# A two-block transformer in one kernel: two-pass gated P times V, gate/up's start and end reordered, context spread, own first buffers for down

## The reference

```
x = x + concat(pool_mixer(u), gla_mixer(q, k, v, g, a), fox_mixer(q, k, v, f)) @ w_o
# fox_mixer: p = softmax(q k^T / 8 + F_t - F_s, causal); o = p @ v   (8 heads of 64)
h = rmsnorm(x, ln2)
gate, up = split(h @ w_gu)              # 1024 -> 2 x 2816
x = x + (silu(gate) * up) @ w_down
x = rmsnorm(x, ln_f)
# second block: adaptive modulation from c, and differential attention over
# 256 context rows (their own modulation) and the 1024 rows of x; final rms norm
```

## Time and profile before

| what | us |
|---|---|
| median of 3 runs | 2244.05 (2243.75 to 2244.96) |
| the profiled execution's own time | 2245.73 |
| its span, first to last instruction | 2243.9 |
| PE busy | 2113.5 (94% of the span) |
| DVE busy | 1384.7 (62%) |
| ACT busy | 1046.0 (47%) |
| POOL busy | 768.8 (34%) |
| mean granted PE clock | 0.977 of full speed |

### The profile page before, as it was taken

The page is one execution under the profiler, slowest core; times in us unless marked ns, Lnnn a source line. Parts: engine busy times, 40 slices in busy tenths (PEclk is TensorE's granted clock), DMA queues, the critical chain, the costliest instruction groups (busy, mean ns, idle before and its releaser), DMA issues. The chain is left out here.

```text
span 2243.9 us, 29580 instructions
## 1 busy us (share of the span) xinstructions
PE 2113.5 (94%) x10092; PEld 1726.2 (77%) x10092; DVE 1384.7 (62%) x1856; ACT 1046.0 (47%) x1677; POOL 768.8 (34%) x503
## 2 busy tenths in 40 slices
PE   6999999988989999989999989999999999999798
PEld 5887777767767888878787868878778787877687
DVE  5545545435577665565445467777867687786864
ACT  4434545445233322322234345566666666665651
POOL 2211222256265554444344533222223122222420
PEclk9999999999999999999999999999999999999899
DMA  3110000004223333243444541111010111102312
GB/s 117 43 38 29 10 28 28 19 19 169 85 85 130 113 122 107 85 144 129 153 148 144 180 174 66 38 38 38 28 51 23 42 42 37 37 28 72 125 66 94
DMA packets 59366, 175.53 MB, mean 78 GB/s; under 512 B 7568, under 2 KB 7984, under 8 KB 59168
## 3 DMA queue, kind: packets, MB, share of 16 engines
q1 hardware_dynamic: 55728, 161.81, 20.7%
q0 software_dynamic: 3568, 12.81, 1.7%
HBM read 144.44 MB, written 29.89 MB: 78 GB/s over the span
## 5 line engine op out<-in xcount | busy, mean ns | idle before, releaser
L2929 ACT ACTIVATE diff_probs<-psum,diff_neg_max 128x1280 f32<-128x1280 f32 x128 | 170.3, 1330 | 121.9 <-DVE diff_neg_max L3159 120.8
L3159 DVE TENSOR_REDUCE diff_neg_max<-psum 128x1 f32<-128x1280 f32 x128 | 189.5, 1486 | 48.7 <-PE psum L2479 48.6
L2538 PE MATMUL psum<-h_hi,w_hi 128*128 128x512 f32 x480 | 193.4, 403 | 7.8 <-DVE h_lo L1523 4.7
L2539 PE MATMUL psum<-h_lo,w_hi 128*128 128x512 f32 x480 | 190.3, 396 | 0.0
L2540 PE MATMUL psum<-h_hi,w_lo 128*128 128x512 f32 x480 | 189.6, 395 | 0.0
L2799 POOL TENSOR_SCALAR diff_probs<-diff_probs,diff_recip 128x1280 f32<-128x1280 f32 x64 | 86.0, 1344 | 268.5 <-DVE diff_probs L3176 268.5
L2210 DVE TENSOR_TENSOR down_a_lo<-down_feat,down_a_hi 128x512 fp32r<-128x512 f32 x42 | 100.1, 2383 | 115.3 <-ACT down_a_hi L2111 114.6
L395 PE MATMUL psum<-h_hi,w_hi 128*128 128x512 f32 x368 | 153.7, 418 | 4.7 <-POOL w_lo L384 2.7
L1651 POOL TENSOR_TENSOR gu_p_lo<-gu_p_whole,gu_p_hi 128x512 fp32r<-128x512 f32 x84 | 125.2, 1513 | 86.3 <-ACT gu_p_hi L1643 86.3
L2478 PE MATMUL psum<-diff_k_hi_lo,diff_q_hi_twice 128*128 128x512 f32 (+1 forms) x384 | 142.8, 372 | 11.6 <-ACT diff_probs L2929 11.5
L1976 POOL TENSOR_TENSOR w_lo<-down_w_raw,w_hi 128x1024 fp32r<-128x1024 f32 x42 | 101.0, 2407 | 140.3 <-ACT w_hi L2109 140.3
(11 more groups left out here) (448 smaller groups left out, 5708.5 us busy)
## 6 DMA issues: line engine op xcount, KB each, us to landing
down_w_raw<-in_w_down SPq DMA_DIRECT2D x44, 512.0 KB, 3.6
gu_w_next<-in_w_gu SPq DMA_DIRECT2D x42, 512.0 KB, 4.2
w_whole<-in_da_w_in SPq DMA_DIRECT2D x30, 512.0 KB, 3.5
gu_ada_w<-in_ada_w SPq DMA_DIRECT2D x24, 512.0 KB, 3.6
w_whole<-in_w_in SPq DMA_DIRECT2D x23, 512.0 KB, 3.4
kept_hid<-gu_hid SPq DMA_DIRECT2D x44, 256.0 KB, 2.1
down_feat<-kept_hid SPq DMA_DIRECT2D x44, 256.0 KB, 4.0
diff_rope_half<-in_rope SPq DMA_DIRECT2D x17, 512.0 KB, 4.1
```

Of the source, the lines that this page charges most:

```text
L2538: pe.matmul(out, wh, rh, start=(k == 0), stop=False)
L2539: pe.matmul(out, wh, rl, start=False, stop=False)
L2929: act.activation(dst, core.psum[:, 1536 * z:1536 * z + NKEY], ACT.Exp, bias=nm[:, qb % 2, z:z + 1], accum_out=rs[:, qb % 2, z:z + 1]).then ...
L3159: dve.tensor_reduce(nm[:, qb % 2, z:z + 1], core.psum[:, 1536 * z:1536 * z + NKEY], AX.X, ALU.max, negate=True).then_inc(s[f"max{z}"], 1)
```

## The change

It has five parts.

1. `times_v` has two matmuls in place of three. v is laid out so that the 128 columns of a head are its 64 hi and 64 lo columns (`v_of`). Both are multiplied with P_hi and with P_lo, so that the product v_lo x P_lo is added. The sum stands in two sets of 64 rows, and `output` copies one and adds the other: a second DVE instruction, with a wait between.
2. Start of gate/up. DVE makes tile 1's weight sums after the rests of the last turn. POOL's order becomes p1, p6, p5, s1, p7, p2, p3, s4, p4. SP stores tile 0 first, then loads tile 2's weights, then the condition rows and the first modulation weights. `cond_silu` moves behind `silu_of_first`; DVE's wait for it moves to tile 2.
3. The context: ACT's eight roundings go to tiles 15, 16 and 17 (3, 3, 2), DVE's to tiles 16, 17 and 18 (2, 3, 3), SP's four stores stand after tile 19.
4. Down's first two weight tiles get buffers of their own, over those of s1 (used by p5), so that ACT rounds them, and DVE takes their features' rests, inside the last tile of gate/up.
5. `add` of token tiles 0 to 2 waits for that token tile's own last matmul (`s_sum`), and no longer for the whole half.

The diff, with most unchanged lines left out:

```diff
@@ -423,7 +423,11 @@
         v_at = next_place(nc)
-        v = [ph.sb(n, [P, NT, P], F32R) for n in ("v_hi", "v_lo")]
+        v = ph.sb("v_hi_lo", [P, 2 * SEQ], F32R)
+        v_parts = v[:, :].rearrange("p (t q m) -> p t q m", t=NT, q=4)
+        v_hi_part = lambda j: v_parts[:, 4 * j:4 * j + 4, 0:4:3, :]
+        v_lo_part = lambda j: v_parts[:, 4 * j:4 * j + 4, 1:3, :]
+        v_of = lambda h, kt: v[:, (2 * kt + h) * P:(2 * kt + h + 1) * P]
...
@@ -481,7 +485,7 @@
-        gates_hi = v[1][:, :, :].rearrange("p t m -> p (t m)")
+        gates_hi = v[:, SEQ:2 * SEQ]
...
@@ -503,7 +507,7 @@
         names = ("parts gates_hi gate_rows k_copied consts_r staged q_hi k_hi q_done k_done v_turned v_hi v_done f_rows "
-                 "scored maxed probs recips scaled pt_turned pt_hi pt_lo pv_done o_read feat_hi")
+                 "scored maxed probs recips scaled pt_turned pt_hi pt_lo pv_done o_rest o_read feat_hi")
...
@@ -735,7 +739,7 @@
                     act.wait_ge(s["v_turned"], 2 * n + j + 1)
-                    act.activation(v[0][:, 4 * j:4 * j + 4, :], ps[PIECE_BANK][:, :].rearrange("p (t m) -> p t m", t=4),
+                    act.activation(v_hi_part(j), ps[PIECE_BANK][:, :].rearrange("p (t h m) -> p t h m", t=4, h=2),
...
@@ -1001,8 +1005,8 @@
                     dve.wait_ge(s["v_hi"], 2 * n + j + 1)
-                    dve.tensor_tensor(v[1][:, 4 * j:4 * j + 4, :], ps[PIECE_BANK][:, :].rearrange("p (t m) -> p t m", t=4),
-                                      v[0][:, 4 * j:4 * j + 4, :].bitcast(F32), ALU.subtract).then_inc(s["v_done"], 1)
+                    dve.tensor_tensor(v_lo_part(j), ps[PIECE_BANK][:, :].rearrange("p (t h m) -> p t h m", t=4, h=2),
+                                      v_hi_part(j).bitcast(F32), ALU.subtract).then_inc(s["v_done"], 1)
...
@@ -1023,8 +1027,11 @@
                     dve.wait_ge(s["pv_done"], nth_pt(i, h, g, nkt[g] - 1) + 3)
-                    r = slice(h * DH, (h + 1) * DH)
-                    dve.tensor_copy(mix[r, 4 + i, g * HALF:(g + 1) * HALF], ps[O_BANK][r, :]).then_inc(s["o_read"], 1)
+                    r, rest = slice(h * DH, (h + 1) * DH), slice((1 - h) * DH, (2 - h) * DH)
+                    out = mix[r, 4 + i, g * HALF:(g + 1) * HALF]
+                    dve.tensor_copy(out, ps[O_BANK][rest, :]).then_inc(s["o_rest"], 1)
+                    dve.wait_ge(s["o_rest"], i * 4 + h * 2 + g + 1)
+                    dve.tensor_tensor(out, ps[O_BANK][r, :], out, ALU.add).then_inc(s["o_read"], 1)
...
@@ -1291,10 +1298,8 @@
                     hi, lo = turned_hi(g, kt)[:, c0:HALF], turned_lo(g, kt)[:, c0:HALF]
-                    pe.matmul(out, v[0][:, kt, :], hi, start=(kt == 0), stop=False)
-                    pe.matmul(out, v[0][:, kt, :], lo, start=False, stop=False)
-                    pe.matmul(out, v[1][:, kt, :], hi, start=False, stop=(kt == nkt[g] - 1))\
-                      .then_inc(s["pv_done"], 1)
+                    pe.matmul(out, v_of(h, kt), hi, start=(kt == 0), stop=False)
+                    pe.matmul(out, v_of(h, kt), lo, start=False, stop=(kt == nkt[g] - 1)).then_inc(s["pv_done"], 1)
...
@@ -1776,6 +1781,8 @@
                         for j, n in enumerate(("hi", "lo")))
+    first_wh, first_wl = (over(f"down_first_w_{n}", [P, 2, D], mix_at + (32 + 8 * j) * 1024, F32R)
+                          for j, n in enumerate(("hi", "lo")))
...
@@ -1851,15 +1858,18 @@
         sync.dma_start(ctx[:, :, :], d["ctx"].rearrange("t p n -> p t n")).then_inc(s_cx, 16)
-        sync.wait_ge(qp.s["prepared"], qp.prepared("s3_lo"))
-        sync.dma_start(cond[:, :, :], d["cond"].partition_broadcast(P)).then_inc(s_cond, 16)
-        load_ada(0)
         qp.store_first(sync, 0)
+        qp.store_second(sync, 0)
...
         def tile(i, last=False):
-            qp.store_second(sync, i - 1)
+            if not (isinstance(i, int) and i == 1):
+                qp.store_second(sync, i - 1)
...
                 qp.load(sync, i + 1)
+            if isinstance(i, int) and i == 1:
+                sync.wait_ge(qp.s["prepared"], qp.prepared("s3_lo"))
+                sync.dma_start(cond[:, :, :], d["cond"].partition_broadcast(P)).then_inc(s_cond, 16)
+                load_ada(0)
...
@@ -1867,15 +1877,14 @@
             tile(i)
-        with sync.Fori(TWICE.stop, CTX_AT + 2) as i:
+        with sync.Fori(TWICE.stop, CTX_AT + 5) as i:
...
             sync.dma_start(d["o_feat"][4 + j, :, :], part.rearrange("p k n -> p (k n)")).then_inc(s_hc_st, 16)
-        with sync.Fori(CTX_AT + 2, LAST_TILE) as i:
-            tile(i)
+        tile(CTX_AT + 5)
...
@@ -1948,7 +1957,7 @@
         whole_rows(6)
-        for q in qp.ORDER[:4]:
+        for q in qp.ORDER[:3]:
...
@@ -1958,9 +1967,13 @@
         rest_s("p5", 2)
+        for q in ("p7", "p2", "p3"):
+            qp.rest_w(pool, 1, q)
         rest_s("p3", 3)
-        qp.rest_w(pool, 1, "p2")
-        with pool.Fori(1, LAST_TILE) as i:
+        qp.rest_w(pool, 1, "p4")
+        for q in qp.ORDER[:5]:
+            qp.rest_w(pool, 2, q)
+        with pool.Fori(2, LAST_TILE) as i:
...
@@ -1971,7 +1984,7 @@
                 for b in range(2):
-                    hi, lo = weights(g, last, b)
+                    hi, lo = weights(g, first, last, b)
...
@@ -1983,9 +1996,10 @@
-    def weights(g, last, b):
-
-        return (last_wh[:, b, :], last_wl[:, b, :]) if g and last else (core.wh[:, b, :], core.wl[:, b, :])
+    def weights(g, first, last, b):
+
+        wh, wl = (last_wh, last_wl) if g and last else (first_wh, first_wl) if first and not g else (core.wh, core.wl)
+        return wh[:, b, :], wl[:, b, :]
...
@@ -2058,6 +2072,8 @@
                 qp.round_w(act, i + 1, "p2")
+            if isinstance(i, int) and i == 1:
+                cond_silu(act)
...
@@ -2073,42 +2089,47 @@
-        def ctx_hi(act):
+        def ctx_hi(act, part):
             act.wait_ge(s_mods, MODS_DONE)
-            for k in range(KT):
+            for k in part:
...
-        tile(1, cond_silu)
+        tile(1)
...
             tile(i)
-        tile(CTX_AT, ctx_hi)
-        with act.Fori(CTX_AT + 1, LAST_TILE) as i:
+        tile(CTX_AT, lambda act: ctx_hi(act, range(0, 3)))
+        tile(CTX_AT + 1, lambda act: ctx_hi(act, range(3, 6)))
+        tile(CTX_AT + 2, lambda act: ctx_hi(act, range(6, KT)))
+        with act.Fori(CTX_AT + 3, LAST_TILE) as i:
             tile(i)
-        tile(LAST_TILE)
+        def first_hi(act):
+            act.wait_ge(s_hc_st, 64)
+            act.wait_ge(qp.s["done"], qp.nth(LAST_TILE, "p5"))
+            for b in range(2):
+                act.wait_ge(loaded[b], 32)
+                act.activation(weights(0, True, False, b)[0], raw[:, b, :], ACT.Copy).then_inc(whi, 1)
+                act.activation(features(0, False, b)[0], feat[:, b, :], ACT.Copy).then_inc(ahi, 1)
+
+        tile(LAST_TILE, first_hi)
...
-        act.wait_ge(s_hc_st, 64)
...
                     n = g * FT + 2 * i + b
-                    hi = features(g, last, b)[0]
                     if g == 0 and first:
-                        act.wait_ge(loaded[b], 32)
-                        act.activation(hi, feat[:, b, :], ACT.Copy).then_inc(ahi, 1)
-                        act.wait_ge(qp.s["done"], qp.nth(LAST_TILE, "p4"))
+                        continue
...
                         act.wait_ge(mm, n + 1)
-                    act.activation(weights(g, last, b)[0], raw[:, b, :], ACT.Copy).then_inc(whi, 1)
-                    if not (g == 0 and first):
-                        act.activation(hi, feat[:, b, :], ACT.Copy).then_inc(ahi, 1)
+                    act.activation(weights(g, first, last, b)[0], raw[:, b, :], ACT.Copy).then_inc(whi, 1)
+                    act.activation(features(g, last, b)[0], feat[:, b, :], ACT.Copy).then_inc(ahi, 1)
...
@@ -2120,8 +2141,10 @@
-        if t >= 4:
-            dve.wait_ge(s_sum, t - 3)
+        if t == 3:
+            dve.wait_ge(mm, FT + 2)
+        else:
+            dve.wait_ge(s_sum, t + 1 if t < 3 else t)
...
@@ -2183,12 +2206,11 @@
             dve.tensor_scalar(yn[:, t % 2, :], y[:, t, :], ss[:, c], None, ALU.mult).then_inc(tr.ready, 1)
-            if t == NT - 1:
-                qp.sums_of_weights(dve, 1)
...
                 tr.dve(dve, t)
+        qp.sums_of_weights(dve, 1)
...
@@ -2241,6 +2263,8 @@
                 qp.second_half(dve, i - 1)
+                if isinstance(i, int) and i == 2:
+                    dve.wait_ge(qp.s["s_hi"], S_HI_COND)
...
@@ -2249,8 +2273,6 @@
                 modulate(first_ada(i) + 1)
-            if first:
-                dve.wait_ge(qp.s["s_hi"], S_HI_COND)
...
@@ -2277,10 +2299,10 @@
-        def ctx_lo(dve):
+        def ctx_lo(dve, part):
...
             dve.wait_ge(s_mods, MODS_DONE)
-            for k in range(KT):
+            for k in part:
...
@@ -2303,13 +2325,14 @@
         tile(CTX_AT)
-        tile(CTX_AT + 1, ctx_lo)
-        with dve.Fori(CTX_AT + 2, LAST_TILE) as i:
+        tile(CTX_AT + 1, lambda dve: ctx_lo(dve, range(0, 2)))
```

(16 more changed lines are left out.)

## The result

The changed kernel took 2217.12 us in the median of 4 executions (2213.17 to 2226.13), the kernel before 2244.51 beside it (2243.75 to 2246.56): ratio 0.9882, 95% interval 0.9848 to 0.9917, 27 us faster. The forecast was 2207 with a range of 2197 to 2220. The profiled execution took 2213.54, its span 2211.6 at a mean clock of 0.983; against the profile before that is 32.3 us less span.

A forecast was written before the change was run, and what follows sets the result against it. TensorE was taken as busy nearly always, leaving fewer matmuls or its waits and the half clock behind them to win. 8.3 + 11.0 + 10.8 + 5.3 + 1.4 = 36.8 off 2244.05 gave 2207 us, range 2197 to 2220.

The forecast's parts named there:

- the 2200 to 2214: Whole kernel: the time range in us given to the forecast itself, chance 0.60.
- two rivals at 2215: Either fox gives nothing (chance 0.15), or gate/up's start keeps its waits and gives 3 us, not 11 (chance 0.10).
- Fox, 8.3: Attention heads: 96 matmuls removed, worth 17.3 us, of which 8.3 reach the end (2 to 14).
- The extra instruction: Fox: the added DVE add takes 0.7 us, mostly hidden, paid once in full before the barrier ending the stage.
- w_o, forecast at nothing: The w_o products after fox: the prediction had no term for them, 0 us.
- The start, 11.0: Start of gate/up: waits for last turn, s3's rest and tile 2's weights go or move, 11.0 us (8 to 14).
- The wait moved to p6: Start of gate/up: a wait of 4 to 5 us before p6, eleven half-clock matmuls costing 2.2, p6 starting 2.8 earlier.
- The context, 10.8: Gate/up's four context tiles: 11.1 us of excess goes except 0.3, giving 10.8 (7 to 11.1).
- Down's start, 5.3: Down's first step loses 8.5 us of excess; 2.7 wait at the third tile and 0.5 clock remain: 5.3 (3 to 6.5).
- The adds, 1.4: End of down's first half: three of four adds go ahead of the last matmul, 1.4 us (0 to 1.5).
- the rivals: Fox nothing 0.15; start keeps waits 0.10; all fox kept, no clock fall, 2196 us, 0.09; slower clock 0.04; within 0.2% 0.02.
- The clock did not fall for whole heads: Fox: rival that half clock stays for whole heads, a pair costing up to 69 us, two giving 2345; chance 0.04.

The follow-up runs named there:

- e6: The changed kernel without VectorE's second instruction for the output of P times V, only the half with v's high part copied: 2217.77 us in one execution.
- e5: The changed kernel with the second matmul of each key tile in P times V issued twice, so three matmuls again: 2225.47 us in one execution.
- e1: The kernel before with only the two-matmul P times V, its layout of v and second output instruction: 2239.0 us, ratio 0.9969.
- e4: The changed kernel with loads for down's third and fourth weight tiles ahead of gate/up's last stores, ln_f and x1 loads behind: 2209.99 us, ratio 0.9838.

## Why the prediction was right, and where it was not

The sign, and the range of 2197 to 2220, held. The forecast of 36.8 us stands against 32.3 in the profiles and 27 in the medians. The median of 2217 lies outside the 2200 to 2214 that I gave 0.60, and inside the range because this was drawn out for two rivals at 2215 that did not come. The total was also helped by misses that offset one another: fox and the start gave more than forecast, w_o and down's start less. In order of the parts:

**Fox, 8.3.** Right in size. The mean of the stage is 305.9 in four traces with three products and 295.15 in nine with two (e6 left aside); less the 1.0 of the gap, 9.8 are won. Kept in the first heads was 1.74 of 2.16, where I had 1.94. In the second heads 1.0 of 2.16 was kept where no half clock disturbs the comparison (38.94 to 37.96), and I had 0.4: part of it is lost there, as said, but less. That it is DVE that takes it was not tested. The profile before also stood on the long side of a scatter of 1.5 us for each change of pair, which I had not reckoned with. The extra instruction cost its 0.7 once, as forecast; the gap grew by 1.0 in all. The page "TensorE: Matmul & The Clock Gate" of the Trainium skill, section Back-to-back issue gap, would have made this term about 5; putting the matmuls back cost 9.8 (e5), so the trace's price stands.

**w_o, forecast at nothing.** The first step that failed. I costed the stage as untouched, but 96 matmuls and their weight loads less are a shorter program for TensorE, and one of its packets of instructions now falls among w_o's first weights. The loss came with the fewer matmuls (e1 has it) and went when they were put back (e5); it was 3.2 in the profile after, and 0 to 3 in others.

**The start, 11.0.** Measured 12.6 (11.3 alone). The wait moved to p6, as said: 4.3 where 4 to 5 was forecast. Counted from the last product of w_o, p6 began 2.65 earlier for my 2.8, with some nine matmuls about 0.42 apart behind it, which cost 1.7 for my 2.2, and tile 2 right behind tile 1. Each of the steps held.

**The context, 10.8.** 11.0 in its own tiles. The stores, of which I wrote that weights a few us late have room, took 1.2 of it back at tile 21, and 0.8 to 3.7 in other executions.

**Down's start, 5.3.** The second step that failed, and the largest: 0.7 was left. The kind was right (the third tile is late behind the last stores and ln_f), the size of its wait was not, with 5.4 and 2.3 of half clock for 2.7 and 0.5. I let its load be issued 4.8 us after down could begin (1079.6 - 1074.8), right behind ln_f's place in the trace before; it came at 6.0 (1048.43 - 1042.39), since VectorE's rests for down, 5.2 us, now stand ahead of the last gatings for which SyncE waits. From the issue to ScalarE's rounding it took 6.1 (1054.56 - 1048.43) for my 3.6: the rounding also waits for the features, whose load was issued 1.4 later and landed 4.6 after that. The 3.6 was the median of 44 loads. At this very place the trace before had 4.4 for the weights and 5.9 for the features, and I did not read it. The rounding and the rest took 3.9 for 3.5. The lower bound of this term, 3, should have gone to 0: the same order that removes a wait lets PE arrive 5.5 earlier at the next one, which does not move.

**The adds, 1.4.** Exact where they stand (99.5 to 98.1). But the second half was longer by about as much: 126.1 in the mean of seven traces against 124.6 in four. The ranges overlap (124.2 to 127.5 and 123.1 to 125.9), so this is likely and not shown. The loads there are held up by the gate row's store, which did not move, and PE now reaches them 1.4 earlier. I had asked what hides the adds, not what comes late behind them.

Of the profiles' 32.3, 1.8 are the scatter of the first stretch. The last 5 us, between 32 in the profiles and 27 in the medians, are not explained by a row: the profiled executions of the changed kernel (2213.5, 2211.1) stood among its shortest, and the others weren't traced. Their lower clocks speak for more half clock, but where it lies stays open.

Of the rivals, none came. The clock did not fall for whole heads in fox: 0.98 in the middle pair, as before. What there is of it, half clock that costs 0 to 2.7 us behind each change of pair, was there before the change too.

## What to carry to other kernels

When a wait goes, look up the next item on the same resource and give it a bound of nothing gained: what is queued behind stores, landings and broadcasts arrives when it did before, and the engine is there sooner. Order the queue by when each transfer is needed, not by when its data were ready; four moved issues were worth 7.7 us of the stretch here, nearly as much as two matmuls in place of three (9.8). And compare stages over several traces before pricing a step of one or two us, since a stage with frequent waits has a scatter of its own.

## What the runs showed of the hardware

- Where a packet of TensorE's instructions, 16 KB, was fetched while weights were loaded, one issue on SyncE took 0.9 to 1.26 us in place of 0.5, the second load landed after 5.6 to 6.1 in place of 4.3 to 4.5, and in four traces of ten the first after 4.7 to 5.0 in place of 3.5. Where the packet fell went with the length of TensorE's program ahead of it (15.9 us ahead of w_o in e5, 2.2 to 2.7 behind its start in nine of the ten with 96 matmuls less). The Trainium skill's page "Runtime: NRT & Kernel Launch", section Instruction fetch mechanics, has these blocks of 16 KiB and calls their cost mostly hidden; the traces agree as to the size, and show a cost where it is not looked for, in another queue's loads.
- A store of 4 KB in packets of 4 bytes delayed loads of 256 KB beside it from about 4 to 9.7 us, and from GpSimd's queue as well as from SyncE's.
- A large VectorE instruction beside a large one of GpSimd took as long as the wait for that and its own work together: the same 128x2048 took 2.3 us by itself, and 6.1 to 6.7 beside GpSimd's rest, ending 2.15 us after it in both traces. Reordering within VectorE moved this cost and did not remove it.
- Behind a wait of 4 to 5 us matmuls at half clock followed each time, and cost 1.6 to 3.0 us behind p6 (ten traces) and 1.5 to 2.9 at down's third tile (seven); without the wait the clock stayed at 1.00 (the windows of e4).
